# The gate's hidden product ahead of a recurrence, and its values centred as they are turned

## The chip, the cores and the metric

One core of one Trainium2 chip runs the whole program in one launch, all in fp32. The metric is the device time of the launch in microseconds, the median of the runs shown. TensorE multiplies into PSUM (8 banks of 128x512), VectorE (DVE in the rows), ScalarE (ACT) and GpSimd (POOL) do the rest, and SyncE (SP) issues the weight transfers.

## The reference, cut to what matters

The program is a hybrid block (attention and a state-space scan), then two mixers with their feed-forward layers. The change touches the first mixer, RWKV-7 time mixing, on a sequence of 512 with 1024 channels and 16 heads of 64:

```python
xx = token_shift(x) - x
xm = x[None] + xx[None] * mix[:, None, None, :]
...
a = jax.nn.sigmoid(a0 + (xa @ a1) @ a2)
g = jax.nn.sigmoid(xg @ g1) @ g2              # g1: 1024 x 160, g2: 160 x 1024
kk = heads(k * k_k); kk = kk / jnp.maximum(jnp.sqrt(jnp.sum(kk * kk, -1, keepdims=True)), 1e-12)
k = k * (1 + (a - 1) * k_a)
_, y = lax.scan(_wkv7_step, state0, xs)       # y is linear in v
mu = y.mean(-1, keepdims=True)                # over the 64 values of a head
var = jnp.square(y - mu).mean(-1, keepdims=True)
y = ((y - mu) * lax.rsqrt(var + GN_EPS)).reshape(B, S, D) * lnx_g + lnx_b
bonus = jnp.sum(rh * kh * r_k, -1, keepdims=True) * vh
y = (y + bonus.reshape(B, S, D)) * g
return y @ w_o
```

## The kernel before, in words

Activations lie with channels on the partitions: a tile is 128 channels (two heads) by 512 tokens, and eight tiles make one activation. Weights stream from HBM through a ring of six slots of 128x1024 (`ring`, filled by `stream`); `weight_used` counts the chunks that TensorE has finished with and so frees slots in order. Each engine runs a list of instructions in program order, and semaphores join the lists. Between stages all engines meet.

The stages around the change, with their places in the profiled execution:

- r, k, v products and the two hidden products of decay and a (to 801 us). `mixed(dst, diff, branch)` makes the mixed input of one branch on VectorE; `hidden_vector` makes those of branches 3 and 4.
- Preparation (801 to 871 us). Rate products (L1696, L1697) on TensorE, sigmoids on ScalarE, the scan of log decays on VectorE; squares of the keys (L1718), their sums per head (L1700), root (L1723), reciprocal (L1755), spread back over the channels by `spread_heads` (L1630), key normalisation (L1758), scaling of k (L1727, L1760); r times k on GpSimd (L1789) and its sums (L1711); then VectorE operations over a whole activation of 128x4096 (L1762 to L1775).
- Recurrence (871 to 1040 us), chunked: eight chunks of 64 tokens in four pairs. For each pair TensorE turns v, k and b (`turn`, L1863), makes Gram tables, inverts by doubling levels, and forms outputs and states.
- Output stage (1040 to 1141 us). Head means by a product with `head_ones` (L2210), centring (L2268), mixing of branch 5 (L1578), the gate's first product (L2216), squares (L2323), sums (L2222), root (L2342), reciprocal (L2284), spreads (L1630), the gate's second product (L2231, copied to SBUF by L2345), scaling (L2287), bonus added by GpSimd (L2317), the gate multiplied in (L2292, L2296), and the output product w_o (L2254 to L2256). The latter splits every operand into a high and a low half (ScalarE rounds, VectorE subtracts) and makes three passes for each of eight banks in each of eight steps k.

The order of the work is the order in the text: nothing is scheduled at run time.

## Time and profile before

| | us |
|---|---|
| Median of 3 runs (lowest 2231.27, highest 5258.97) | 2231.93 |
| Profiled execution, its time | 2228.96 |
| Its span | 2227.2 |
| TensorE busy in it | 2046.6 (92%) |
| VectorE busy in it | 1298.4 (58%) |
| ScalarE busy in it | 812.3 (36%) |
| GpSimd busy in it | 238.0 (11%) |

The span runs from the first to the last instruction; the time of the execution has 1.8 us more around it. The highest of the three runs is the first one, and the median is not moved by it. Busy shares are averages over stages that are bound by different engines, so they say little of one stage.

### The profile page before, as it was taken

What the parts mean: (1) busy time and instruction counts of PE and PEld (TensorE: products, weight loads), DVE (VectorE), ACT (ScalarE), POOL (GpSimd) and SP (SyncE); (2) the same over time, 40 slices, a digit from 0 to 9 for tenths busy, and PEclk for the clock granted to TensorE, in tenths of its full rate; (3) what the DMA queues carried; (4) which work ended last, traced back from release to release, by engine and by line L of the source; (5) the groups of instructions that cost most, each with busy time, mean ns of one, the idle gap of its engine ahead of it and who ended that gap; (6) DMA issues with size and microseconds to landing.
All of it is one profiled execution on the core that took longest, in us unless ns stands there. A gap on an engine that the chain in (4) does not pass through costs nothing. (4 is left out here: it accounts for less than half of the span.)

```text
span 2227.2 us, 31380 instructions
## 1 busy us (share of the span) xinstructions
PE 2046.6 (92%) x13270; PEld 1546.9 (69%) x13270; DVE 1298.4 (58%) x1845; ACT 812.3 (36%) x1171; POOL 238.0 (11%) x164
## 2 busy tenths in 40 slices
PE   7999989999979973898999999999939899999998
PEld 3877867887858832786567888885516567888885
DVE  2345756666545478676457776434585457666534
ACT  3454654444233362232242222322326533222322
POOL 0000003334410021003200000000035200000000
PEclk9998999999989997999899999999979999999999
DMA  7223002211313210000112222222200022223221
GB/s 281 95 85 105 1 10 69 83 58 58 94 58 112 89 44 1 4 4 21 38 57 101 99 95 95 95 96 82 94 35 1 3 74 85 95 95 101 93 100 38
DMA packets 47019, 158.26 MB, mean 71 GB/s; under 512 B 5328, under 2 KB 7504, under 8 KB 46880
## 3 DMA queue, kind: packets, MB, share of 16 engines
q1 hardware_dynamic: 45296, 151.84, 20.7%
q10 hardware_dynamic: 1584, 4.43, 0.6%
q8 instruction: 105, 1.72, 0.3%
q14 instruction: 34, 0.28, 0.0%
HBM read 154.10 MB, written 2.14 MB: 70 GB/s over the span
## 5 line engine op out<-in xcount | busy, mean ns | idle before, releaser
L1006 PE MATMUL banks<-up_x_high,up_w_high 128*128 128x512 f32 x1056 | 411.5, 390 | 8.4 <-DVE up_w_low L1000 3.8
L1008 PE MATMUL banks<-up_x_high,up_w_low 128*128 128x512 f32 x1056 | 411.0, 389 | 0.0
L1007 PE MATMUL banks<-up_x_low,up_w_high 128*128 128x512 f32 x1056 | 410.9, 389 | 0.0
L1000 DVE TENSOR_TENSOR up_w_low<-weight_ring,up_w_high 128x1024 fp32r<-128x1024 f32 x132 | 161.6, 1225 | 268.6 <-ACT up_w_high L995 268.6
L995 ACT CAST up_w_high<-weight_ring 128x1024 fp32r<-128x1024 f32 x132 | 138.2, 1049 | 362.3 <-PE banks L1008 338.2
L1006 PEld LDWEIGHTS banks<-up_x_high,up_w_high 128*128 128x128 f32 x1056 | 198.2, 188 | 53.2 <-issue 11.6
L1008 PEld LDWEIGHTS banks<-up_x_high,up_w_low 128*128 128x128 f32 x1056 | 198.2, 188 | 41.4
L1007 PEld LDWEIGHTS banks<-up_x_low,up_w_high 128*128 128x128 f32 x1056 | 198.3, 188 | 40.9
L1542 POOL TENSOR_TENSOR hproj_w_low<-weight_ring,hproj_w_high 128x1024 fp32r<-128x1024 f32 x43 | 106.0, 2466 | 498.8 <-ACT hproj_w_high L1342 498.8
L1061 DVE SCALAR_TENSOR_TENSOR act<-banks,cols,act 128x511 f32<-128x511 f32 (+1 forms) x176 | 131.8, 749 | 6.2
L1217 PE MATMUL banks<-hproj_x_high,hproj_w_high 128*128 128x512 f32 x224 | 90.0, 402 | 5.2 <-DVE hproj_x_low L1493 3.4
L425 PE MATMUL banks<-rkv_x_high,rkv_w_high 128*128 128x512 f32 x192 | 75.7, 394 | 13.5 <-DVE rkv_x_low L496 13.3
L1219 PE MATMUL banks<-hproj_x_high,hproj_w_low 128*128 128x512 f32 x224 | 87.9, 393 | 0.0
L1218 PE MATMUL banks<-hproj_x_low,hproj_w_high 128*128 128x512 f32 x224 | 87.9, 392 | 0.0
L1103 ACT ACTIVATE act<-act 128x512 f32<-128x512 f32 x44 | 27.8, 632 | 161.1 <-DVE act L1061 161.1
L449 DVE TENSOR_TENSOR qkv_w_low<-weight_ring,qkv_w_high 128x1024 fp32r<-128x1024 f32 x24 | 29.4, 1225 | 87.3 <-ACT qkv_w_high L445 87.3
L1342 ACT CAST hproj_w_high<-weight_ring 128x1024 fp32r<-128x1024 f32 x44 | 46.0, 1047 | 93.3 <-PE banks L1325 54.4
L426 PE MATMUL banks<-rkv_x_low,rkv_w_high 128*128 128x512 f32 x192 | 75.4, 393 | 0.0
L427 PE MATMUL banks<-rkv_x_high,rkv_w_low 128*128 128x512 f32 x192 | 75.3, 392 | 0.0
L1058 DVE TENSOR_SCALAR act<-banks,cols 128x512 f32<-128x512 f32 x88 | 70.8, 805 | 0.0
L449 DVE TENSOR_TENSOR rkv_w_low<-weight_ring,rkv_w_high 128x1024 fp32r<-128x1024 f32 x24 | 29.3, 1225 | 61.3 <-ACT rkv_w_high L445 61.3
L2641 PE MATMUL banks<-stat,act 128*128 128x128 f32 (+3 forms) x96 | 32.7, 490 | 34.3 <-PEq L2409 27.1
(476 smaller groups left out, 4005.1 us busy)
## 6 DMA issues: line engine op xcount, KB each, us to landing
weight_ring<-in_up SPq DMA_DIRECT2D x88, 512.0 KB, 3.2
weight_ring<-in_down SPq DMA_DIRECT2D x44, 512.0 KB, 3.2
weight_ring<-in_w_ada SPq DMA_DIRECT2D x24, 512.0 KB, 4.5
weight_ring<-in_w_rkv SPq DMA_DIRECT2D x24, 512.0 KB, 3.5
weight_ring<-in_w_in SPq DMA_DIRECT2D x20, 512.0 KB, 3.5
weight_ring<-in_w_out SPq DMA_DIRECT2D x16, 512.0 KB, 3.6
weight_ring<-in_w_q SPq DMA_DIRECT2D x8, 512.0 KB, 5.4
weight_ring<-in_w_k SPq DMA_DIRECT2D x8, 512.0 KB, 3.5
```

What stands on the lines that cost most here:

```text
L425: nc.tensor.matmul(PS[:, n, :], high, x_high[:, parts[s] % slots, :], start=k == 0, stop=False)
L426: nc.tensor.matmul(PS[:, n, :], high, x_low[:, parts[s] % slots, :], start=False, stop=False)
L995: nc.scalar.copy(w_high[:, n % 2, :], ring[:, i % RING, :]).then_inc(wh_made, 1)
L1000: nc.vector.tensor_tensor(w_low[:, n % 2, :], ring[:, i % RING, :], w_high[:, n % 2, :].bitcast(f32), ALU.subtract).then_inc(wl_made, 1)
L1006: nc.tensor.matmul(PS[:, bank, :], high, x_high[:, k, :], start=start, stop=False)
L1007: nc.tensor.matmul(PS[:, bank, :], high, x_low[:, k, :], start=False, stop=False)
L1008: return nc.tensor.matmul(PS[:, bank, :], low, x_high[:, k, :], start=False, stop=stop)
L1061: nc.vector.scalar_tensor_tensor(out=dst(n)[:, j:], in0=PS[:, n % 4, 0:T - j], scalar=w_col(n, taps - 1 - j), in1=dst(n)[:, j:], op0=ALU.m ...
L1217: nc.tensor.matmul(PS[:, bank, :], high, x_high[:, k, :], start=k == 0, stop=False)
L1218: nc.tensor.matmul(PS[:, bank, :], high, x_low[:, k, :], start=False, stop=False)
L1219: return nc.tensor.matmul(PS[:, bank, :], low, x_high[:, k, :], start=False, stop=k == 7)
L1542: nc.gpsimd.tensor_tensor(w_low[:, t % 2, :], ring[:, (first + 1 + t) % RING, :], w_high[:, t % 2, :].bitcast(f32), ALU.subtract).then_inc ...
```

## The change

- The mixed input of branch 5 is made in place of `xx`, behind the mixings of branches 3 and 4. The gate's first product runs in the preparation, behind the key sums; its result goes, unactivated, into the two ring slots that held its weights, and stays there over the recurrence. These slots are given free by the first two gate tiles of the output stage.
- `xx` is also `bonus`, so the squares of the keys get three buffers of their own, and their sums alternate with the rate products. ScalarE's gains wait for the product step that reads what they overwrite. VectorE scales all of k first and normalises the keys after. GpSimd's eight `rk_ones` tables wait for the key sums, since they share memory with the squares' buffers.
- When v is turned, the transposes become products with a matrix that subtracts the mean over each head, so that the recurrence's outputs have mean zero. The means and centring of the output stage go.
- In the output stage the gate is multiplied into y by VectorE from PSUM, ahead of the root, and into the bonus by GpSimd; GpSimd's addition is the last step. The head selector for the square sums is fetched at the recurrence's start.

```diff
-        "pairs64_1", "pairs64_2", "ident64"]
+        "pairs64_1", "pairs64_2", "ident64", "centre"]
...
-           "flip": p + f == P - 1, "neg_after": np.where(f > p, NEG, 0)}
+           "flip": p + f == P - 1, "neg_after": np.where(f > p, NEG, 0), "centre": (p == f) - (p // HD == f // HD) / HD}
...
             for k in range(8):
                 mixed(a_, xx, 3)(k).then_inc(mix_w, 1)
                 mixed(xm, xx, 4)(k).then_inc(mix_a, 1)
+            for k in range(8):
+                mixed(xx, xx, 5)(k)
...
+        gate_step, gate_hidden, gate_kept = sem("gate7_hidden_step"), sem("gate7_hidden_made"), sem("gate7_hidden_kept")
+        hid_g = [ring[0:80, (at["used"] + n) % RING, 0:T] for n in range(2)]
+        key_squares = [late[:, 0:T], late[:, T:2 * T], stat[:, 1, :]]
...
+                def key_sum(n):
+                    pe.wait_ge(key_sq, n + 1)
+                    nc.tensor.matmul(PS[:, 0, :], to_all_groups(n), key_squares[n % 3], start=n == 0, stop=n == 7).then_inc(key_sums, 1)
...
-                for n in range(8):
-                    pe.wait_ge(key_sq, n + 1)
-                    mm = nc.tensor.matmul(PS[:, 0, :], to_all_groups(n), bonus[:, n, :], start=n == 0, stop=n == 7)
-                mm.then_inc(key_sums, 1)
-                pe.wait_ge(inverted, 2)
+                    if n:
+                        key_sum(n - 1)
+                key_sum(7)
+                for n in range(2):
+                    i = at["used"] + n
+                    pe.wait_ge(weight_loaded[i % RING], 16 * (i // RING + 1))
...
+                for k in range(8):
+                    for n in range(2):
+                        mm = nc.tensor.matmul(PS[0:80, 6 + n, :], ring[:, (at["used"] + n) % RING, k * 80:(k + 1) * 80], bonus[:, k, :], start=k == 0, stop=k == 7)
+                    mm.then_inc(gate_step, 1)
+                pe.wait_ge(inverted, 2)
                 for n in range(8):
+                    if n >= 6:
+                        pe.wait_ge(gate_kept, n - 5)
                     spread_heads(n, n).then_inc(spread, 1)
...
-                    nc.scalar.activation(bonus[:, n, :], kk[:, n, :], ACT.Square).then_inc(key_sq, 1)
+                    if n >= 3:
+                        act.wait_ge(key_sums, n - 2)
+                    nc.scalar.activation(key_squares[n % 3], kk[:, n, :], ACT.Square).then_inc(key_sq, 1)
...
-                act.wait_ge(key_sums, 1)
+                act.wait_ge(key_sums, 8)
...
                 for n in range(8):
+                    act.wait_ge(gate_step, n + 1)
                     nc.scalar.activation(bonus[:, n, :], a_[:, n, :], ACT.Identity, scale=col("k_a", n), bias=rest_of_gain[:, n:n + 1]).then_inc(gain_less, 1)
+                for n in range(2):
+                    nc.scalar.copy(hid_g[n], PS[0:80, 6 + n, :]).then_inc(gate_kept, 1)
...
-                act.wait_ge(ends, 1)
...
                 for n in range(8):
+                    dve.wait_ge(gain_less, n + 1)
+                    nc.vector.tensor_tensor(kx[:, n, :], bonus[:, n, :], kx[:, n, :], ALU.mult).then_inc(k_scaled, 1)
+                for n in range(8):
                     dve.wait_ge(spread, n + 1)
                     nc.vector.tensor_tensor(kk[:, n, :], kk[:, n, :], PS[:, n, :], ALU.mult).then_inc(key_unit, 1)
-                    dve.wait_ge(gain_less, n + 1)
-                    nc.vector.tensor_tensor(kx[:, n, :], bonus[:, n, :], kx[:, n, :], ALU.mult).then_inc(k_scaled, 1)
...
+                dve.wait_ge(ends, 1)
...
+                pool.wait_ge(key_sums, 8)
                 for n in range(8):
                     nc.gpsimd.tensor_scalar(rk_ones[:, n * P:(n + 1) * P], mat("head_ones"), col("r_k", n), None, ALU.mult).then_inc(ones_made, 1)
...
-                        mm = nc.tensor.transpose(PS[:, turn_bank(i, n) + p // 4, p % 4 * P:(p % 4 + 1) * P], pair_of(t, i)[:, p, :], mat("ident"))
+                        dst = PS[:, turn_bank(i, n) + p // 4, p % 4 * P:(p % 4 + 1) * P]
+                        if n == 0:
+                            mm = nc.tensor.matmul(dst, pair_of(t, i)[:, p, :], mat("centre"), start=True, stop=True)
+                        else:
+                            mm = nc.tensor.transpose(dst, pair_of(t, i)[:, p, :], mat("ident"))
...
+            @block.sync
+            def _(sp):
+                sp.dma_start(of_heads_late, A["of_heads"]).then_inc(of_in, 16)
...
-                for n in range(8):
-                    nc.tensor.matmul(PS[:, n, :], mat("head_ones"), yy[:, n, :], start=True, stop=True).then_inc(mean_made, 1)
-                pe.wait_ge(gn_centred, 8)
...
-                for k in range(8):
-                    pe.wait_ge(mixed_g, k + 1)
-                    for n in range(2):
-                        mm = nc.tensor.matmul(PS[0:80, 1 + n, :], g[n][:, k * 80:(k + 1) * 80], mix_g[:, k, :], start=k == 0, stop=k == 7)
-                        if k == 7:
-                            mm.then_inc(weight_used, 1)
-                pe.wait_ge(heads_in, 80)
+                pe.wait_ge(of_in, 16)
                 for n in range(8):
                     pe.wait_ge(gn_squared, n + 1)
-                    mm = nc.tensor.matmul(PS[:, 0, :], to_all_groups(n), sq[n], start=n == 0, stop=n == 7)
+                    mm = nc.tensor.matmul(PS[:, 0, :], of_heads_late[:, 2 * (KT - n):2 * (KT - n) + P], sq[n], start=n == 0, stop=n == 7)
...
                 def gate_tile(n):
                     if n >= 4:
                         pe.wait_ge(gate_moved, n - 3)
+                        pe.wait_ge(gn_gated, n - 3)
                     for j in range(2):
-                        mm = nc.tensor.matmul(PS[:, 3 + n % 4, :], g2_[j][:, n * P:(n + 1) * P], hid_g[j], start=j == 0, stop=j == 1)
+                        mm = nc.tensor.matmul(PS[:, 3 + n % 4, :], g2_[j][:, n * P:(n + 1) * P], act_g[j], start=j == 0, stop=j == 1)
+                        if j == 0 and n < 2:
+                            mm.then_inc(weight_used, 1)
...
                 pe.wait_ge(gn_inverted, 1)
+                pe.wait_ge(heads_in, 64)
...
-                    spread_heads((0, 1, 2, 7)[n % 4], n).then_inc(gn_spread, 1)
+                    spread_heads(SPREAD_BANK[n % 4], n).then_inc(gn_spread, 1)
...
                         gate_tile(5 + n // 4 * 2)
...
                         elif k == 0:
                             pe.wait_ge(gate_moved, n + 2)
+                            pe.wait_ge(gn_gated, n + 2)
...
-                nc.vector.tensor_tensor(diff[:, :, 1:T], x[:, :, 0:T - 1], x[:, :, 1:T], ALU.subtract).then_inc(differed, 1)
-                nc.vector.tensor_scalar(diff[:, :, 0:1], x[:, :, 0:1], -1.0, None, ALU.mult).then_inc(differed, 1)
-                for n in range(8):
-                    dve.wait_ge(mean_made, n + 1)
-                    nc.vector.scalar_tensor_tensor(out=yy[:, n, :], in0=PS[:, n, :], scalar=-1.0 / HD, in1=yy[:, n, :],
-                                                   op0=ALU.mult, op1=ALU.add).then_inc(gn_centred, 1)
-                dve.wait_ge(differed, 2)
-                for k in range(8):
-                    mixed(mix_g, diff, 5)(k).then_inc(mixed_g, 1)
...
+                def times_gate(n):
+                    dve.wait_ge(gate_moved, n + 1)
+                    dve.wait_ge(gn_squared, n + 1)
+                    if n >= 6:
+                        dve.wait_ge(gn_scaled, n + 1)
+                    nc.vector.scalar_tensor_tensor(out=yy[:, n, :], in0=PS[:, 3 + n % 4, :], scalar=col("lnx_g", n), in1=yy[:, n, :],
+                                                   op0=ALU.mult, op1=ALU.mult).then_inc(gn_gated, 1)
+
+                def times_root(n):
+                    dve.wait_ge(gn_spread, n + 1)
+                    if n < 6:
+                        dve.wait_ge(gn_gated, n + 1)
+                    nc.vector.tensor_tensor(yy[:, n, :], yy[:, n, :], PS[:, SPREAD_BANK[n % 4], :], ALU.mult).then_inc(gn_scaled, 1)
...
-                for n in range(8):
-                    dve.wait_ge(gn_spread, n + 1)
-                    nc.vector.scalar_tensor_tensor(out=yy[:, n, :], in0=yy[:, n, :], scalar=col("lnx_g", n), in1=PS[:, (0, 1, 2, 7)[n % 4], :],
-                                                   op0=ALU.mult, op1=ALU.mult).then_inc(gn_scaled, 1)
-                    if n >= 2:
-                        dve.wait_ge(gn_shifted, n - 1)
-                        dve.wait_ge(gate_moved, n - 1)
-                        nc.vector.tensor_tensor(yy[:, n - 2, :], yy[:, n - 2, :], gate[:, n - 2, :], ALU.mult).then_inc(gated, 1)
-                for n in range(6, 8):
-                    dve.wait_ge(gn_shifted, n + 1)
-                    dve.wait_ge(gate_moved, n + 1)
-                    nc.vector.tensor_tensor(yy[:, n, :], yy[:, n, :], gate[:, n, :], ALU.mult).then_inc(gated, 1)
-                    if n == 6:
-                        low_of_input(0)
+                for n in range(4):
+                    times_gate(n)
+                for n in range(4):
+                    times_root(n)
+                times_gate(4)
+                times_gate(5)
+                for n in range(4, 8):
+                    times_root(n)
+                low_of_input(0)
+                times_gate(6)
+                times_gate(7)
                 low_of_input(1)
...
-                for n in range(8):
+
+                def gate_bonus(n):
                     pool.wait_ge(bonus_shifted, n + 1)
+                    pool.wait_ge(gate_moved, n + 1)
+                    nc.gpsimd.tensor_tensor(bonus[:, n, :], bonus[:, n, :], gate[:, n, :], ALU.mult).then_inc(bonus_gated, 1)
+
+                def add_bonus(n):
+                    pool.wait_ge(bonus_gated, n + 1)
                     pool.wait_ge(gn_scaled, n + 1)
-                    nc.gpsimd.tensor_tensor(yy[:, n, :], yy[:, n, :], bonus[:, n, :], ALU.add).then_inc(gn_shifted, 1)
+                    pool.wait_ge(gn_gated, n + 1)
+                    nc.gpsimd.tensor_tensor(yy[:, n, :], yy[:, n, :], bonus[:, n, :], ALU.add).then_inc(gated, 1)
+
+                for at0, at1 in ((0, 4), (4, 6), (6, 8)):
+                    for n in range(at0, at1):
+                        gate_bonus(n)
+                    for n in range(at0, at1):
+                        add_bonus(n)
...
-                    act.wait_ge(gn_centred, n + 1)
                     nc.scalar.activation(sq[n], yy[:, n, :], ACT.Square, scale=HD ** -0.5).then_inc(gn_squared, 1)
...
+                def move_gate(n):
+                    act.wait_ge(gate_out, n + 1)
+                    nc.scalar.copy(gate[:, n, :], PS[:, 3 + n % 4, :]).then_inc(gate_moved, 1)
+
+                for n in range(2):
+                    nc.scalar.activation(act_g[n], hid_g[n], ACT.Sigmoid).then_inc(hid_g_taken, 1)
+                act.wait_ge(hid_g_taken, 2)
+                act.wait_ge(gn_eps, 1)
                 high_of_weights(0)
                 high_of_weights(1)
-                act.wait_ge(weight_used, first_g + 2)
-                for n in range(2):
-                    nc.scalar.activation(hid_g[n], PS[0:80, 1 + n, :], ACT.Sigmoid).then_inc(hid_g_taken, 1)
-                act.wait_ge(gn_eps, 1)
                 act.wait_ge(gn_sums, 1)
                 nc.scalar.activation(head_sums, PS[:, 0, :], ACT.Sqrt, bias=small[:, 250:251]).then_inc(gn_rooted, 1)
-                for n in range(8):
-                    act.wait_ge(gate_out, n + 1)
-                    nc.scalar.copy(gate[:, n, :], PS[:, 3 + n % 4, :]).then_inc(gate_moved, 1)
+                for n in range(6):
+                    move_gate(n)
                 high_of_input(0)
+                move_gate(6)
+                move_gate(7)
                 high_of_input(1)
...
-                for dst, src, landed in ((of_heads, A["of_heads"], heads_in), *((t, A["to_heads"], heads_in) for t in to_heads),
-                                         (g2_[0], A["w_g2"][0:80, :], g2_in), (g2_[1], A["w_g2"][80:160, :], g2_in)):
+                for dst, src, landed in ((g2_[0], A["w_g2"][0:80, :], g2_in), (g2_[1], A["w_g2"][80:160, :], g2_in),
+                                         *((t, A["to_heads"], heads_in) for t in to_heads)):
```

## Rows read from the trace of the kernel before

**Rows 1.** The table by stretch, us of the span: each engine's busy time (instructions), clock, DMA.
```profile
801.20:816.70 15.50, 12.27 (x41) 4.67 (x42) 13.65 (x19) 14.91 (x26) 7.47 (x8) 1.00 0.15 60
...
842.50:871.00 28.50, 2.73 (x4) 0.50 (x2) 28.04 (x18) 3.76 (x2) 5.38 (x1) 0.59 0.00 0
...
900.00:1039.90 139.90, 124.58 (x4200) 112.46 (x4201) 91.68 (x140) 42.55 (x63) 8.28 (x8) 1.00 0.02 4
...
1094.00:1100.00 6.00, 5.91 (x14) 4.73 (x15) 1.04 (x2) 0.00 (x0) 0.00 (x0) 0.50 0.01 3
```

**Rows 2.** Timeline of TensorE: start, us, line, tiles, count, idle before and its releaser.
```profile
1039.93 7.11 PE L2210 MATMUL banks<-act,squares 128*128 128x512 f32 x16 [0.93 <-PEq L1843]
1050.47 13.93 PE L2216 MATMUL banks<-act,weight_ring 128*80 128x512 f32 x32 [3.44 <-DVE act L1578]
...
1071.10 7.03 PE L2231 MATMUL banks<-act 80*128 80x512 f32 x16
1078.06 1.14 PE L1630 MATMUL banks<-aux 16*128 16x512 f32 x8
...
1082.77 2.24 PE L1630 MATMUL banks<-aux 16*128 16x512 f32 x8
1084.94 5.87 PE L2231 MATMUL banks<-act 80*128 80x512 f32 x8
1094.09 0.77 PE L2254 MATMUL banks<-w_o_x_high,w_o_w_high 128*128 128x512 f32 x1 [3.29 <-DVE w_o_x_low L2279]
```

**Rows 3.** Timeline of ScalarE in the same stretch.
```profile
1045.51 1.83 ACT L2323 ACTIVATE aux<-act 128x512 f32<-128x512 f32 x3 [5.89 <-DVE act L2268]
...
1050.23 1.98 ACT L2329 CAST w_o_w_high<-weight_ring 128x1024 fp32r<-128x1024 f32 x2
1052.22 1.28 ACT L2339 ACT_TABLE_LOAD   x1
...
1072.64 0.69 ACT L2342 ACTIVATE aux<-banks,small 128x512 f32<-128x512 f32 x1
```

**Rows 4.** Groups by line between 1039.9 and 1094 us: count, busy us, mean ns, idle before.
```profile
L2313 POOL TENSOR_SCALAR w_out_act<-w_out_act,cols 128x512 f32<-128x512 f32 x8 | 19.8, 2496 | 5.1 <-POOLq L1843 5.1
...
L2287 DVE SCALAR_TENSOR_TENSOR act<-act,cols,banks 128x512 f32<-128x512 f32 x8 | 5.7, 738 | 2.5 <-PE banks L1630 2.5
...
L2275 DVE TENSOR_TENSOR w_o_w_low<-weight_ring,w_o_w_high 128x1024 fp32r<-128x1024 f32 x2 | 2.8, 1420 | 0.0
```

**Rows 5.** Single lines of GpSimd in the whole span: duration min/median/max in ns.
```profile
L2313 POOL TENSOR_SCALAR w_out_act<-w_out_act,cols x8: 1556/2072/5803, 1039.9 to 1057.1; 128x512 f32<-128x512 f32 x8
...
L2317 POOL TENSOR_TENSOR act<-act,w_out_act x8: 1267/1712/1728, 1080.1 to 1091.0; 128x512 f32<-128x512 f32 x8
```

**Rows 6.** Timeline of VectorE before the recurrence.
```profile
794.79 0.75 DVE L1578 SCALAR_TENSOR_TENSOR act<-w_out_act,cols,act 128x512 f32<-128x512 f32 x1
...
822.45 3.35 DVE L1755 RECIPROCAL aux<-aux 128x512 f32<-128x512 f32 x1
...
829.77 1.39 DVE L1760 TENSOR_TENSOR act<-w_out_act,act 128x512 f32<-128x512 f32 x1
...
842.44 4.41 DVE L1762 TENSOR_TENSOR w_out_act<-w_out_act,act 128x4096 f32<-128x4096 f32 x1
846.77 1.27 DVE L1764 COPY late<-rkv_act 128x64 f32<-128x64 f32 x1
```

**Rows 7.** Timelines of ScalarE, TensorE and GpSimd before the recurrence.
```profile
800.33 0.58 ACT L1662 COPY aux<-banks 64x512 f32<-64x512 f32 x1
...
815.89 0.79 ACT L1721 ACTIVATE w_out_act<-banks,cols 128x512 f32<-128x512 f32 x1
...
812.85 7.13 PE L1700 MATMUL banks<-w_out_act,aux 128*128 128x512 f32 x16
...
829.34 1.27 POOL L1789 TENSOR_TENSOR w_out_act<-act 128x512 f32<-128x512 f32 x1 [20.56 <-DVE act L1760]
```

**Rows 8.** Timeline of TensorE at the recurrence's first turn.
```profile
875.02 1.09 PE L1863 MATMUL banks<-squares,act 128*128 128x128 f32 x8
```

26 lines of the change are left out of this document (13 added, 13 removed).

## The prediction

> **What bounds the kernel now.** I read the table by stretch first. The recurrence (900 to 1040 us) is TensorE's: 124.6 us busy of 139.9 at a clock of 1.00. The stretch ahead of it (842.5 to 871 us) is VectorE's, 28.04 us of 28.5 [rows 1]. Between recurrence and output product I then followed TensorE's timeline, and there the reader is to see a chain rather than one busy engine: the head means at 1039.93, the gate's first product from 1050.47 for 13.93 us, the square sums behind it, four gate tiles at 1071.10, head spreads at 1078.06 and 1082.77, the last gate tiles at 1084.94, and the first output matmul at 1094.09 after 3.29 us of waiting for VectorE's low half of the input [rows 2]. That is 1094.09 - 1039.93 = 54.2 us. TensorE's order is fixed, so what stands ahead of the square sums delays root, reciprocal and all else. Nothing runs beside this chain that could fill it, so a cut of the chain shows in full at the end.
>
> **The output stage after the change (the gain).** I walk through it from 1039.9.
> ScalarE can square at once, since the values arrive centred: 8 x 0.60 (three take 1.83) ends at 1044.7; then a table load of 1.28, two sigmoids of about 0.55 straight from the ring, 1047.1; two weight halves, 1.98, 1049.1; a second table load, 1.28, and the root, 0.69: 1051.1 [rows 3].
> TensorE sums squares as they come, one 128x512 sum being two passes of 7.11/16 = 0.444 us: 8 x 0.87 from 1040.6 is 1047.5. Four gate tiles at 7.03/4 = 1.76 end at 1054.5 [rows 2].
> VectorE has nothing to do until the halves are there: two low halves of 1.42 on average end at 1051.2, and the reciprocal, 3.35, ends at 1054.6 [rows 4, 6]. It meets TensorE just as gate tile 3 ends. The first four spreads take 1.1 [rows 2]: 1055.7.
> VectorE then makes four gate products and four root products. Both read one operand from PSUM, as L2287 does (0.74 each, issued every 0.65) [rows 4]: gate products to 1057.2, root products to 1059.7. TensorE meanwhile makes gate tiles 4 and 5 to 1059.2, spreads 4 to 7 to 1060.7 (the last waits for root product 3), gate tiles 6 and 7 to 1064.2. VectorE's products 4, 5 and roots 4 to 7 end at 1063.3.
> GpSimd gets a job that decides more than before: eight shifts, eight products of bonus and gate (moved to it), eight additions. Shifts at the uncontended 1.56 take until 1052.4, and 1 us more for the two low halves: 1053.4. A product or addition takes 1.27 when nothing competes, 1.71 when VectorE does [rows 5]. At 1.3, four products end at 1058.6 and the first addition at 1059.9; ScalarE rounds it (0.6), and VectorE's low half follows its last root product, 1063.3 + 0.6 to 1.3. Everything is late together: the output product starts at about 1064.5. For k = 1, 2, 3 GpSimd is ready by 1064, for 4 and 5 by 1069, for 6 and 7 by 1075; the product needs them over 5 us apart (24 passes of at least 5.91/28 = 0.21) [rows 1], so only the first counts. At 1.71 the start is 1.4 to 2 us later.
> So 1094.1 - 1064.5 = 29.6 us. What is late next is TensorE itself, then VectorE. Removed and paid in this sum: means, centring, mixing (VectorE) and the 13.93 us product. DMA moves: the two gate weights are issued ahead of the head selectors instead of behind, and land well before 1047; ring slots come free at gate tile 0, some 15 us earlier than now, so no weight chunk is later.
> **The clock there.** Today it has fallen by the last gate tiles (four passes per tile, 5.87 us for two tiles against 3.5) and is 0.50 for the first 6 us of the output product [rows 1, 2]: the level of 1.2 GHz. The 14 passes there took 5.9 us; at 2.4 GHz they take half, so 2.9 are lost. The light spell ahead of the fall (spreads, 2.24 us with a wait) is 1.6 us in the new order and follows another as now. I call the clock even: the fall costs 2.4 on the tiles (start 1067) and the 2.9 stay; no fall gives the 2.9 back. Ends 27.2 and 32.5, I take 29.
>
> **Ahead of the recurrence (a cost).** VectorE's eight more mixings go behind 794.79: 8 x 0.66 ends at 800.8, while ScalarE's last copy of that stage ends at 800.91 [rows 6, 7]. Free by 0.1 us; without that cover at most 5.3.
> Key sums now alternate with the rate products, 0.87 + 0.86 on TensorE per tile, against ScalarE's three operations every 1.68; ScalarE ends this loop at 816.7 [rows 7]. The squares wait for a buffer three tiles back, which TensorE frees about 1.8 us early. The sums end near 816.4 instead of 820, but VectorE is busy to 822 with the scans and the centring, and its reciprocal starts at 822.45 [rows 6]: nothing gained, up to 1 lost if the loop drags.
> The gate product, 13.93 us, runs from 816.7 to 830.6 on a TensorE that idles there. Behind it wait ScalarE's eight gains (they overwrite its input; the last 831.2) and the spreads; behind the gains, VectorE's eight key products. VectorE is at 825.8 then, and it is not held by them alone: GpSimd multiplies each scaled key at once. The row pair to see: GpSimd's L1789 runs 829.34 to 830.61, and VectorE's L1760, issued at 829.77, takes 1.39 instead of 0.69, ending 0.55 behind it [rows 6, 7]. The two exclude each other. Today VectorE's PSUM product of 0.6 hides under GpSimd's, so the pair costs 1.9 and eight end at 842.4. After: key products alone lock step with GpSimd at 1.27 + 0.6 = 1.87, ending near 838.5; then eight PSUM products of 0.6, 843.3, under which GpSimd ends. Copy L1764 no longer waits for GpSimd (1.27 to 0.25) [rows 6]. Balance 0.9 - 1.0 = 0. If instead VectorE runs through before GpSimd gets in, it is held by the gains only: 831.8, then 836.6, 5.8 earlier.
> GpSimd's r_k tables, eight in 7.47 us [rows 1], move from under the scans to 816.4, beside VectorE's centring, as long as L1762's 4.41: one wait of 0.93 ahead of it and one behind, or none. I take +1 for this stage; ends -6 and +5.
> The Trainium skill bears here (SBUF — State Buffer, "SBUF: two separate sides"): VectorE with two SBUF inputs and a GpSimd operation that reads SBUF take a shared port pair, whole instructions long; with one SBUF input outside its two-port modes VectorE does not contend. This trace agrees: 0.74 for L2287 with GpSimd busy [rows 4]. A rule that each GpSimd operation blocks is against this change, which adds eight; my fourth case prices it.
>
> **In the recurrence (a cost).** 32 transposes, eight in each of four turns, become products with the centring matrix. Eight transposes take 1.09 [rows 8]. Two passes of 128 columns, from 0.444 for 512, are 0.22: eight take 1.78. +0.7 to 0.8 per turn, 3.0 if TensorE's chain carries all, 0 if slack does (it idles 15 of 139.9 us) [rows 1]. I take 2.3; should weight loads not overlap, 4 x 3 = 12 is the far end. The selector's DMA is issued at the recurrence's start on an idle queue, 72 KB: 0. The matrix makes the constants 64 KB longer, fetched behind the early ones: 0 to 0.3. Dropping ScalarE's wait for the chunk ends frees it 7 us early, for nobody.
>
> **Sum.** -29 + 1 + 2.3 = -25.7. On the profiled execution, 2228.96 us: 2203.3. The median of the runs is 2231.93, 3 above it: 2206.
>
> **The rivals.** (1) Clock kept and VectorE never locked: 2231.9 - 32.5 - 3 + 2.3 = 2199; for it, TensorE has no gap over 1 us in my walk; against it, today's fall after the same pattern. (2) The clock falls early: all four late gate tiles at 1.2 GHz, 3.5 each. Then 1055.7 + 7.0 + 2.2 + 7.0 = 1072, 22 gained, 3.3 and perhaps 3 lost: 2213 to 2216. (3) Centring costs its far end, 12 in place of 2.3: 2216. (4) The other side, slower than before: GpSimd's port. If every GpSimd operation stopped VectorE for its whole length ahead of the recurrence (7.5 + 8 x 1.27 = 17.7, and the last held for 4.4 by a long one of VectorE's, 22.1), and took 2.5 in the output stage, as the shifts do today, the start would be 1040 + 13 x 2.5 + 1.3 = 1073.8, 20.3 gained: 2231.9 - 20.3 + 22.1 + 2.3 = 2236 [rows 4]. It decides once stalls take over 26 us in all; against it, L1760's loss is half of a GpSimd operation today. (5) The change gives nothing because something else ends the stage, such as weights in the ring: 2232 to 2235; against it, the slots free earlier.
>
> **How the numbers follow.** Forecast 2206 (2201 to 2211) 0.47; (1) 0.19; (2) 0.18; (3) 0.07; (4) 0.04; (5) 0.05. The range 2195 to 2219 takes in both ends of the clock and nearly all of the port question, and leaves out (4), (5). Two per cent, 44.6 us, is about what a measurement of this kernel can tell from no change; no case reaches it, as even 32.5 + 6 is 1.7%. Faster by more 0.02, within 0.96, slower by more 0.02.
>
> **What would show it.** Output matmul 24 to 30 us after the recurrence's end instead of 54; square sums done 7.6 after it; reciprocal and gate tile 3 ending together; GpSimd's first addition at about +20. Turn 0 of each pair at 1.8 instead of 1.09. Key products in steps of about 1.87. I am wrong if the first output matmul waits for GpSimd, if the clock row behind the last spreads is 0.5, or if VectorE stands idle between 826 and 845.

## The result and the profile after

| | before | changed |
|---|---|---|
| Median, us (runs) | 2231.6 (4) | 2205.07 (4) |
| The changed kernel's runs | | 2195.43, 2200.32, 2209.82, 2212.37 |
| Ratio, 95% interval | | 0.9879 [0.9857, 0.9902] |
| Profiled execution, span | 2228.96, 2227.2 | 2200.32, 2198.5 |

The change gains 1.2%: the median falls by 26.5 us to 2205.07 (forecast 2206). One thing of the table is odd: 39 more runs of the kernel before, made beside the experiments, lie in one group from 2227.3 to 2236.3; the four of the changed kernel span 17 us, in two pairs. The profiled execution is one of the lower pair.

The table by stretch of the changed kernel (ahead of the recurrence, recurrence, output stage up to the output product, output product, all that follows) answers to [rows 1]:

```profile
799.60:868.10 68.50, 42.97 (x112) 15.00 (x112) 64.98 (x55) 33.27 (x42) 22.17 (x16) 0.81 0.04 14
869.40:1040.60 171.20, 152.07 (x4864) 136.10 (x4864) 109.66 (x166) 52.38 (x76) 8.30 (x8) 0.98 0.02 4
1040.60:1064.80 24.20, 23.38 (x64) 9.49 (x64) 15.88 (x20) 15.17 (x23) 24.13 (x17) 1.00 0.31 81
1064.80:1107.80 43.00, 42.97 (x190) 35.62 (x191) 19.07 (x21) 10.51 (x14) 11.55 (x8) 1.00 0.26 86
...
1107.80:2198.50 1090.70, 1024.49 (x4286) 767.92 (x4284) 641.44 (x1042) 365.52 (x564) 58.82 (x69) 0.97 0.23 76
```

The output stage is TensorE's now, busy 23.38 of 24.2 us at a clock of 1.00, and GpSimd is busy for 24.13 of them. Measured between the same instructions, in us of each profiled execution (1.5 us lie between the stretch and the recurrence, in both):

| | before | changed | difference |
|---|---|---|---|
| start of the stretch ahead of the recurrence | 801.2 | 799.6 | -1.6 |
| that stretch | 69.0 | 68.3 | -0.7 |
| recurrence | 168.3 | 171.3 | +3.0 |
| its end to the first output matmul | 54.1 | 24.1 | -30.0 |
| output product | 45.7 | 43.0 | -2.7 |
| all that follows, untouched | 1087.4 | 1090.7 | +3.3 |

The sum is -28.7. The last row is instructions that nobody changed: over the thirteen profiled executions of this document it lies between 1087.2 and 1091.5, so its +3.3 is scatter from one execution to the next; here it goes with the clock, 0.98 before and 0.97 after over the same 4286 matmuls. The first row holds the eight added mixings on VectorE, which end at 799.24, just ahead of ScalarE's last copy at 799.31. The stretch begins between 797.2 and 801.5 in the profiled executions without these mixings and between 797.4 and 801.4 in those with them, so this row is scatter too, and the rows that the change touched add up to -30.4.

TensorE's timeline of the output stage, beside [rows 2], whose first output matmul stood 54.2 us behind the first row:

```profile
1041.41 2.81 PE L2245 MATMUL banks<-aux,late 128*128 128x512 f32 x6 [1.68 <-ACT aux L2366]
1044.06 1.88 PE L2245 MATMUL banks<-late 128*128 128x512 f32 x4
...
1048.35 7.03 PE L2255 MATMUL banks<-act 80*128 80x512 f32 x16
1055.31 1.14 PE L1630 MATMUL banks<-aux 16*128 16x512 f32 x8
1056.38 3.70 PE L2255 MATMUL banks<-act 80*128 80x512 f32 x8
1060.01 1.14 PE L1630 MATMUL banks<-aux 16*128 16x512 f32 x8
1061.08 3.70 PE L2255 MATMUL banks<-act 80*128 80x512 f32 x8
1064.83 0.47 PE L2282 MATMUL banks<-w_o_x_high,w_o_w_high 128*128 128x512 f32 x1
```

Means and gate product are gone from it; no row waits except the first; the last gate tiles take 3.70 where they took 5.87, and the first output matmul 0.47 where it took 0.77. Those two are the clock that stayed up. VectorE and GpSimd in the same stretch:

```profile
1051.41 3.35 DVE L2318 RECIPROCAL aux<-aux 128x512 f32<-128x512 f32 x1
...
1063.79 0.78 DVE L2299 TENSOR_TENSOR w_o_x_low<-act,w_o_x_high 128x512 fp32r<-128x512 f32 x1
```
```profile
1040.67 13.51 POOL L2344 TENSOR_SCALAR w_out_act<-w_out_act,cols 128x512 f32<-128x512 f32 x8 [4.54 <-POOLq L1867]
1054.15 4.96 POOL L2349 TENSOR_TENSOR w_out_act<-w_out_act 128x512 f32<-128x512 f32 x4
1059.07 4.96 POOL L2355 TENSOR_TENSOR act<-act,w_out_act 128x512 f32<-128x512 f32 x4
1063.99 2.98 POOL L2349 TENSOR_TENSOR w_out_act<-w_out_act 128x512 f32<-128x512 f32 x2
```

The low part of the input (L2299) is the last thing that the output product needs from another engine. Here it ends at 1064.57, 0.2 us before TensorE is through with its gate tiles, so nothing waits. It reads two tiles of the core's memory and starts 0.24 us before one run of GpSimd operations ends. Keep this pair of rows in mind: the experiments trace the two groups of times to it.

### The profile page after: what moved, and what is told of

Its sections match the earlier page's. It is cut to its first block and busy times, and to the rows that moved or that the text cites. A ratio compares the mean times of both kernels' runs of the same rounds, so it can differ in the third digit from the quotient of the medians.

```text
span 2198.5 us, 31439 instructions
## 1 busy us (share of the span) xinstructions
PE 2038.5 (93%) x13286; PEld 1547.9 (70%) x13286; DVE 1282.0 (58%) x1835; ACT 814.6 (37%) x1173; POOL 242.7 (11%) x172
```

## The experiments

"Stage" is the time from the recurrence's end to the first output matmul. Times are medians; the profiled execution has the stretches.

| kernel | us (lowest to highest, runs) | recurrence | stage | output product |
|---|---|---|---|---|
| gate half alone | 2204.15 (2203.53 to 2205.47, 4) | 166.5 | 34.0 | 42.9 |
| centring half alone | 2229.27 (2223.95 to 2236.21, 10) | 170.9 | 51.2 | 45.8 |
| the same, sums first | 2232.95 (2229.21 to 2234.86, 10) | 171.2 | 51.7 | 45.4 |
| mean not subtracted | 2197.68 (2194.38 to 2208.34, 4) | 166.4 | 26.7 | 43.0 |
| before, TensorE kept busy | 2236.61 (2227.6 to 2244.74, 10) | 168.0 | 67.6 | 43.3 |
| query x key on VectorE | 2207.9 (2197.43 to 2209.1, 4) | 171.4 | 31.4 | 45.3 |
| shifts twice | 2221.76 (2221.36 to 2223.28, 4) | 171.5 | 43.8 | 45.9 |
| shifts early | 2203.89 (2203.36 to 2205.17, 4) | 173.7 | 26.5 | 43.0 |
| pauses | 2200.72 (2197.46 to 2204.09, 4) | 172.1 | 24.1 | 43.0 |
| pauses, query x key on VectorE | 2199.78 (2198.32 to 2201.11, 4) | 169.7 | 25.6 | 42.9 |
| pauses, spare products | 2202.31 (2200.68 to 2203.89, 4) | 170.0 | 24.1 | 43.0 |

### The two halves of the change

The gate half alone: transposes as before, means by products, centring by VectorE in the output stage.

```diff
-                        if n == 0:
-                            mm = nc.tensor.matmul(dst, pair_of(t, i)[:, p, :], mat("centre"), start=True, stop=True)
+                for n in range(8):
+                    nc.tensor.matmul(PS[:, n, :], mat("head_ones"), yy[:, n, :], start=True, stop=True).then_inc(mean_made, 1)
+                pe.wait_ge(gn_centred, 8)
```

> Only the first half of the change: the gate's hidden product is made ahead of the recurrence, v is turned by transposes as before, and the head means and their subtraction are back in the output stage. Theory (the output stage is one chain, and each piece counts by its place in it): TensorE makes the means for 7.1 us, squares follow VectorE's centring, and the square sums end about 14.2 us into the stage instead of 7.7; everything behind moves by the same 6.5 to 7, so the stage from its start to the first output matmul takes about 31 us (24.2 with the whole change, 54.2 before), and the recurrence is back at 168.2 us. The median is about 4 us above that of the whole change, near 2209. Rival (the two halves cover each other: with the product gone, the means fall under waits that exist anyway): the stage stays within 1 us of 24.2 and the time falls by 3 us against the whole change, since only the cost in the recurrence goes.

The centring half alone, on the kernel before:

```diff
-                for n in range(8):
-                    nc.tensor.matmul(PS[:, n, :], mat("head_ones"), yy[:, n, :], start=True, stop=True).then_inc(mean_made, 1)
-                pe.wait_ge(gn_centred, 8)
+                        if n == 0:
+                            mm = nc.tensor.matmul(dst, pair_of(t, i)[:, p, :], mat("centre"), start=True, stop=True)
```

> Only the second half of the change: v is centred as it is turned, the means and their subtraction are gone from the output stage, and the gate's hidden product stays there. Theory (chain): the product now waits for VectorE's difference, 4.43 + 0.57, and the first mixing instead of the centring, so it starts about 5.7 us into the stage instead of 10.5 and all behind it moves by 4.9; the stage takes 49.3 us, the recurrence 171.2, and the sum is about -2 us against before. Rival (means and centring are worth their own length, 7.1 + 4.9 us): stage near 42 us, about -9 us in all.

TensorE in the first:

```profile
1035.80 8.80 PE L2241 MATMUL banks<-act,squares 128*128 128x512 f32 x16 [0.93 <-PEq L1867]
1045.43 2.81 PE L2246 MATMUL banks<-aux,late 128*128 128x512 f32 x6 [0.83 <-issue]
```

and in the second:

```profile
1044.33 15.72 PE L2217 MATMUL banks<-act,weight_ring 128*80 128x512 f32 x32 [6.82 <-DVE act L1578]
```

The gate half carries the gain: stage 34.0 against 54.1. By the medians it carries all of it: 2204.15 against the whole change's 2205.07, both 0.9879 of before, and not the 4 us more that were expected. Its four runs lie within 1.9 us, where the whole change's fall in two groups.

The means take 8.80 us here (7.11 in [rows 2]), for they begin at the low clock; less those 1.7 us the stage is 32.3, where the first theory gave 31.

The centring half by itself gives 2.9 us in the output stage and takes 2.6 in the recurrence: its ratio to before is 0.999 [0.9976, 1.0005]. The gate product comes only 4.7 us sooner after the recurrence (5.8 for 10.5) and, after TensorE has idled 6.82 us, runs its first part at the low clock, 15.72 us for 13.93. Nothing that is removed ahead of VectorE's mixing pays while the gate product waits for that mixing.

In the stage the two halves are worth more together: once the gate product is gone, centring takes it from 34.0 to 24.1, and pays 4.8 of these 9.9 us back in the recurrence (166.5 against 171.3). The profiled spans differ by 3.6 (2202.1 and 2198.5), no more than the scatter of the last row; in the changed kernel's median even this is lost to its upper group.

Could the centring half pay by another order? Square sums and root ahead of the gate product and its sigmoid, on the centring half alone:

```diff
+                    mm = nc.tensor.matmul(PS[:, 0, :], to_all_groups(n), sq[n], start=n == 0, stop=n == 7)
                 for k in range(8):
                     pe.wait_ge(mixed_g, k + 1)
...
-                    mm = nc.tensor.matmul(PS[:, 0, :], to_all_groups(n), sq[n], start=n == 0, stop=n == 7)
```

> As centre_only, and TensorE makes the square sums ahead of the gate's hidden product, with ScalarE's root ahead of its sigmoids. Theory (a good part of the change's gain is the order, which frees root and reciprocal, not the work moved): the sums end 7.7 us into the stage, the reciprocal is ready at about 15 instead of 37, but the gate tiles still wait for the product (21.5) and the sigmoids, so the stage is then product, eight gate tiles of 1.76, spreads: 21.5 + 2 + 14 + 2 + some 3 of additions, about 41 to 43 us. That would be 7 us better than centre_only by the order alone. Rival (the work moved is all that counts): the stage stays within 1 us of centre_only's 49.

```profile
1047.24 5.35 PE L2216 MATMUL banks<-aux 128*128 128x512 f32 x6 [5.02 <-DMA aux<-in_to_heads]
...
1056.72 13.90 PE L2222 MATMUL banks<-act,weight_ring 128*80 128x512 f32 x32
1071.78 3.70 PE L2232 MATMUL banks<-act 80*128 80x512 f32 x8 [1.17 <-ACT act L2338]
```

No: the ratio is 1.0008 [0.9998, 1.0017], and the theory's 41 to 43 us for the stage fell. The sums wait 5.02 us for the head selectors' transfer, begin at the low clock, and push the gate product to 1056.72, so that the gate tiles begin at 1071.78. That is 28.6 us behind the recurrence's end, as in the centring half alone (28.3), and from there both need 23 more. The changed kernel avoids both: it loads one selector in the recurrence, and has no gate product there.

### What centring costs

The changed kernel with transposes in the turns; the mean is then never subtracted, and the output is another one.

> The changed kernel with transposes in place of the centring products when v is turned, so the mean over a head is not subtracted at all: the output differs, the number of instructions in the output stage does not. Theory (TensorE's chain carries the centring in full): the recurrence takes 168.2 us instead of 171.2, every other stage is as in the changed kernel, and the median is 3 us lower, near 2202. Rival (something else took the 3 us, such as a stall of the new queue at the recurrence's start): the recurrence stays above 170.5 us.

TensorE at the first turn of values in the changed kernel (eight products, each two instructions), and at the next turn, eight transposes as ever:

```profile
872.98 2.05 PE L1889 MATMUL banks<-squares,act 128*128 128x128 f32 x16
...
876.87 1.09 PE L1891 MATMUL banks<-squares,act 128*128 128x128 f32 x8
```

Four such turns are 4 x 0.96 = 3.8 us. The recurrences agree in size: seven kernels with centring (those of the table but two, which add work at its start, and the changed kernel) take 169.7 to 172.1, mean 171.2; four without (before, before kept busy, gate half, mean not subtracted) 166.4 to 168.3, mean 167.3. The difference of the means is 3.9, but it mixes two kinds of kernel. With the gate product in its old place centring costs some 3 us (168.2 to 171.1, two kernels each); with the product moved ahead it costs some 4.7 (166.5 to 171.2, two against five).

TensorE's busy time in the recurrence, by the same table of stretches, is 151.74 on average with centring and 147.26 without, 4.5 more. So centring costs some 3 to 5 us, about the TensorE time that it adds, and how much of that time slack hides isn't shown. The stage of this kernel is 26.7 because its square sums began at the low clock (4.48 us for the first six instructions, where the changed kernel takes 2.81) and because its low part took 1.69, for which TensorE waited 0.96:

```profile
1034.33 4.48 PE L2242 MATMUL banks<-aux,late 128*128 128x512 f32 x6 [1.68 <-ACT aux L2363]
...
1060.33 0.47 PE L2279 MATMUL banks<-w_o_x_high,w_o_w_high 128*128 128x512 f32 x1 [0.96 <-DVE w_o_x_low L2296]
```

### Whether the clock was the gain

On the kernel before, spare products after head spreads 4 to 7 and ahead of the output product:

```diff
                     spread_heads((0, 1, 2, 7)[n % 4], n).then_inc(gn_spread, 1)
+                    if n >= 4:
+                        pe.wait_ge(gate_moved, 5)
+                        nc.tensor.matmul(PS[:, 3, :], mat("ones"), squares[:, 0:T], start=True, stop=True)
...
+                for _ in range(4):
+                    nc.tensor.matmul(PS[:, 3, :], mat("ones"), squares[:, 0:T], start=True, stop=True)
```

> The kernel before, with spare products (their results are never read) that keep TensorE busy while it waits for gate tiles and ahead of the output product; nothing of the change is in it. Theory: part of what the change gained, 5.3 us, was not work removed but the granted clock kept at 1.00, which fell before in gate tiles 6 and 7 (5.87 us each where others take 3.5 to 3.7) and in the first blocks of the output product (45.7 us where 43.0 is its length at full clock). With the pauses filled the output product takes 43.0 and the whole gets 3 to 5 us shorter than before: 2227 to 2229. Rival: the clock fell for another reason than the pauses, then tiles 6 and 7 still take 5.87 and the whole is within 1 us of before, or above it, since the spare products cost 0.2 to 0.4 each.

The granted clock is the third number from the end of each row; then TensorE:

```profile
1070.00:1080.00 10.00, 10.00 (x30) 4.15 (x29) 5.50 (x5) 4.40 (x7) 1.39 (x2) 1.00 0.00 0
1080.00:1090.00 10.00, 10.00 (x16) 2.44 (x14) 8.03 (x9) 0.82 (x2) 8.59 (x6) 0.73 0.01 2
1090.00:1095.00 5.00, 5.00 (x7) 1.73 (x7) 1.35 (x2) 0.00 (x0) 2.38 (x2) 0.50 0.00 0
```
```profile
1082.30 1.13 PE L2243 MATMUL banks<-squares 128*128 128x512 f32 x2
...
1088.22 2.07 PE L2243 MATMUL banks<-squares 128*128 128x512 f32 x2
...
1094.09 7.03 PE L2231 MATMUL banks<-act 80*128 80x512 f32 x8
```

The theory fell as it was put: the time is 1.0019 [1.0001, 1.0037] of before. TensorE had no pause between 1080 and 1095 by the records, and the granted clock sank to 0.50 (1.2 GHz) all the same. At that level the spare products, 2.07 each, stood on the path and the stage took 67.6. The output product did take 43.3 instead of 45.7, since by its second matmul the clock was back (0.40 each, where the kernel before began with 0.63). So 2.4 us of it do hang on the clock, and 42.9 to 43.3 stands in every row of the table whose clock is up there. Why it sank while TensorE was busy I leave open; only its consequence is shown.

### The two groups of times

These runs began with another aim, the port that VectorE and GpSimd share. The eight products of query and key on VectorE, between its key products:

```diff
-                    nc.gpsimd.tensor_tensor(bonus[:, n, :], r[:, n, :], kx[:, n, :], ALU.mult).then_inc(rk_made, 1)
...
+                    nc.vector.tensor_tensor(bonus[:, n, :], r[:, n, :], kx[:, n, :], ALU.mult).then_inc(rk_made, 1)
```

> The changed kernel with the eight products of query and key (the first factor of the bonus) made by VectorE between its own key products in place of GpSimd. Theory: in the stretch ahead of the recurrence VectorE and GpSimd hinder each other while both read and write the core's memory; the key products took 1.43 each beside GpSimd, and with GpSimd silent they take about 0.6 to 0.7 and the added ones as much, so that 16 operations take 10 to 11 us where 8 took 11.45: the stretch ends 0.5 to 2 us earlier, and the whole gains as much. Rival: they don't hinder each other and 1.43 is the operation's own length: then 16 take 22 us and the stretch gets 10 us longer.

Ahead of the recurrence the theory held: sixteen products end at 834.67, where eight took from 824.94 to 836.39, each 0.68 once GpSimd's last table (its L1818, until 825.93) is out of the way; the stretch takes 66.7 instead of 68.3. But the stage took 31.4. VectorE, GpSimd and TensorE there:

```profile
1062.16 8.09 DVE L2304 TENSOR_TENSOR w_o_x_low<-act,w_o_x_high 128x512 fp32r<-128x512 f32 x1
1070.18 1.40 DVE L2311 SCALAR_TENSOR_TENSOR act<-banks,cols,act 128x512 f32<-128x512 f32 x2
```
```profile
1057.41 4.97 POOL L2360 TENSOR_TENSOR act<-act,w_out_act 128x512 f32<-128x512 f32 x4
1062.34 2.49 POOL L2354 TENSOR_TENSOR w_out_act<-w_out_act 128x512 f32<-128x512 f32 x2
1064.78 2.48 POOL L2360 TENSOR_TENSOR act<-act,w_out_act 128x512 f32<-128x512 f32 x2
1067.22 2.48 POOL L2354 TENSOR_TENSOR w_out_act<-w_out_act 128x512 f32<-128x512 f32 x2
1071.09 2.97 POOL L2360 TENSOR_TENSOR act<-act,w_out_act 128x512 f32<-128x512 f32 x2 [1.38 <-DVE act L2311]
```
```profile
1070.51 0.77 PE L2287 MATMUL banks<-w_o_x_high,w_o_w_high 128*128 128x512 f32 x1 [7.36 <-DVE w_o_x_low L2304]
```

The low part took 8.09 us instead of 0.78. It was issued at 1062.16, 0.2 us before one GpSimd operation ended, and got in neither there nor between any of the next six, whereas the changed kernel's, issued 0.24 us before the same operation's end, did get in; it ended at 1070.25, 0.55 us after GpSimd ran out of work at 1069.70, and GpSimd had run out only because its next addition needed VectorE's L2311, which stood behind the low part.

The output product starts 7.3 us late and, TensorE having idled 7.36 us, at the low clock (0.77 for the first matmul): 45.3 for 43.0. Together that is 9.6 us, most of the distance between this kernel's one run at 2197.43 and its three at 2207.8 to 2209.1; the changed kernel's two pairs stand 13.2 apart, more than this stall by itself gives. This is the only profile of an upper run.

Each of these low parts ends 0.55 us behind the end of some GpSimd operation: in the changed kernel, the gate half, the shifts made early and the kernel whose mean isn't subtracted behind the first that ends after it was issued (0.78 or 1.7 us in all), here behind the seventh. So the change from one GpSimd operation to the next is sometimes met and sometimes not; what decides it isn't shown.

GpSimd's shifts made twice, so that its row of work is 12.3 us longer (the norm's shift is then in the output twice):

```diff
+                pool.wait_ge(bonus_shifted, 8)
+                for n in range(8):
+                    nc.gpsimd.tensor_scalar(bonus[:, n, :], bonus[:, n, :], col("lnx_b", n), None, ALU.add).then_inc(bonus_shifted, 1)
...
-                    pool.wait_ge(bonus_shifted, n + 1)
+                    pool.wait_ge(bonus_shifted, n + 9)
```

> The changed kernel with GpSimd's eight shifts of the bonus made twice over (so the norm's shift is added twice to the output). They take 13.5 us for eight beside VectorE in the output stage. Theory: the first gated addition, which the output product waits for by way of its input, ended some 3 us ahead of need, so another 12.5 to 13.5 us of GpSimd delay the output product by about 10: from the end of the recurrence to it 33 to 35 us in place of 24.2, and the whole 9 to 11 us longer. This tells how near the changed kernel stands to the next bound. Rival: the gated additions are far from the path; the stage keeps its 24.2 and the time is that of the changed kernel.

```profile
1073.73 10.85 DVE L2299 TENSOR_TENSOR w_o_x_low<-act,w_o_x_high 128x512 fp32r<-128x512 f32 x1 [9.51 <-ACT w_o_x_high L2380]
```

The low part was ready to start at 1073.73, 32.7 us after the recurrence: the slack theory's 33. Then it stood 10.85 us. GpSimd worked without a gap from 1041.02 to 1084.03; the low part ended at 1084.58, 0.55 us behind it, as before. So the stage was 43.8 and not 33 to 35, and the median 16.7 us above the changed kernel's and not 9 to 11: the theory had the slack right and no stall in it. The four runs lie within 1.9 us, which fits a stall in each of them; one was profiled.

The shifts at the recurrence's start, where GpSimd idles:

```diff
             def _(pool):
+                for n in range(8):
+                    nc.gpsimd.tensor_scalar(bonus[:, n, :], bonus[:, n, :], col("lnx_b", n), None, ALU.add).then_inc(bonus_shifted, 1)
                 for c in range(NCH):
...
-                for n in range(8):
-                    nc.gpsimd.tensor_scalar(bonus[:, n, :], bonus[:, n, :], col("lnx_b", n), None, ALU.add).then_inc(bonus_shifted, 1)
```

> The changed kernel with GpSimd's eight shifts made at the recurrence's start, where GpSimd is idle, in place of the output stage. Theory: GpSimd isn't what bounds the output stage now, TensorE's square sums and gate tiles are, so the stage stays within 0.5 us of 24.2 and the whole within 1 us of the changed kernel, unless VectorE, less hindered in the output stage, makes the centre shorter by up to 2 us. Rival: the stage hangs on GpSimd, and gets 3 us or more shorter; or the shifts hinder VectorE at the recurrence's start, and the first 15 us of the recurrence get 1 to 3 us longer.

The stage isn't GpSimd's: it got no shorter. That it is 26.5 us and not within 0.5 of 24.2 comes from square sums at the low clock (1.5 more) and a wait of 0.95 for the first low part. The four runs lie within 1.8 us. GpSimd now waits for gate tiles between its first products, but the row in which the low part is issued (1067.78) has no pause from 1061.50 on; it took 1.68 us and got in at the next change of operation. The recurrence takes 2.4 us longer than the changed kernel's (173.7): VectorE's products at its start, beside the shifts, are 0.8 of it, and the granted clock over its first 24 us is 0.79 where that kernel has 0.86.

Then the direct test, with nothing taken from GpSimd but three pauses:

```diff
                 def gate_bonus(n):
+                    if n in (4, 6):
+                        pool.wait_ge(xol_made, n // 2 - 1)
...
                 def add_bonus(n):
+                    if n == 6:
+                        pool.wait_ge(xol_made, 3)
```

> The changed kernel in which GpSimd stops three times until VectorE has made a low part of the output product's input: before the gatings 4 and 6 and before the additions of tiles 6 and 7. Nothing is taken away. Theory: the changed kernel's runs fall in two groups (2195 and 2200, 2210 and 2212) since VectorE's first low part, which reads two tiles in the core's memory, has to find a gap in a row of GpSimd operations without a pause; where it misses it, it stands for 8 to 11 us (0.7 by itself), the output product starts 7 us late and at half the clock. With a pause made for it every run finds it: all within 5 us, median 2195 to 2201, stage 24 to 25 us. Rival: the two groups come from something else (the clock, transfers): then they stay, with a median at 2203 to 2210.

```profile
1065.19 0.78 DVE L2299 TENSOR_TENSOR w_o_x_low<-act,w_o_x_high 128x512 fp32r<-128x512 f32 x1
```
```profile
1060.44 4.97 POOL L2359 TENSOR_TENSOR act<-act,w_out_act 128x512 f32<-128x512 f32 x4
1066.05 2.54 POOL L2351 TENSOR_TENSOR w_out_act<-w_out_act 128x512 f32<-128x512 f32 x2 [0.63 <-DVE w_o_x_low L2299]
```

GpSimd waits 0.63 us, the stage keeps its 24.1, and no run is in the upper group: 2197.46 to 2204.09, ratio 0.9858 [0.9843, 0.9873]. Counted over kernels: without pauses in GpSimd's row (the changed kernel, mean not subtracted, query x key on VectorE) 6 of 12 runs are in an upper group at 2207.8 to 2212.4; with pauses 0 of 12 are. The 4.4 us at the median are less certain, since the two ratios' intervals overlap.

Two things keep this from being the whole account. The gate half and the kernel with the shifts early have an unbroken row at their low part too, and none of their 8 runs is in an upper group. And the runs of the centring half lie over 12 us and those of the kernel kept busy over 17 us, though the low parts in their profiles take 0.68 and 0.69 us; where that scatter comes from wasn't looked into. The pauses remove a stall that is seen in two traces, and with it, as far as 12 runs can tell, the upper group; the stall isn't seen in an upper run of the changed kernel itself.

The two other kernels with the pauses. With the query-key products on VectorE:

> The same pauses of GpSimd, and the eight products of query and key made by VectorE in place of GpSimd as in the run before, where the stretch ahead of the recurrence took 66.7 us in place of 68.3 while the output stage had the long stall. Theory: the stall goes and the 1.6 us stay: median 1 to 2.5 us under that of the kernel with the pauses alone, 2194 to 2199. Rival: without the stall the two are equal, because the clock at the recurrence's start takes the 1.6 us back.

The stretch ahead keeps its 66.7, the stall is gone, and the four runs lie at 2198.32 to 2201.11, ratio 0.9856 [0.9839, 0.9872]. The 0.9 us at the median are less than four runs can tell. The stage is 25.6 because the first six square sums take 4.40 us, at the low clock again, and the recurrence is 2.4 shorter than with the pauses alone; neither was sought. Its median is the lowest of the kernels here whose output is right.

With spare products ahead of the recurrence:

```diff
+                pe.wait_ge(prepared, 5)
+                pe.wait_ge(bonus_made, 1)
+                for _ in range(5):
+                    nc.tensor.matmul(PS[:, 0, :], mat("ones"), squares[:, 0:T], start=True, stop=True)
```

> The kernel with the pauses, and five spare products on TensorE between its last work ahead of the recurrence and the recurrence's first products (it idled 22.7 us there and began at a granted clock of 0.50, held for some 3.5 us). Theory: the recurrence begins at the full clock and its first products take half: 1 to 2 us less in the recurrence, the median 1 to 2 us under that of the kernel with the pauses alone. Rival: the gain is nothing, as the clock dips at 883 to 890 us come earlier or deeper, or the spare products run into the start and delay it by up to 1 us.

```profile
865.77 7.33 PE L1732 MATMUL banks<-squares 128*128 128x512 f32 x10 [17.16 <-DVE w_out_act L1804]
874.35 0.29 PE L1881 MATMUL banks<-act,w_out_act 64*64 64x128 f32 x1 [1.24 <-PEq L1837]
```

The first products take 0.29 instead of 0.44, so the clock was up, and the recurrence is 2.1 shorter than with the pauses alone. But the spare products, at the low clock at first, end at 873.1, and the recurrence starts 3.1 later than it would have. The rival held: nothing gained, with a delay of 3.1 us where it allowed for 1.

## Why the prediction was right, and where it was not

**The output stage (-29).** Right in its parts and its sum: 24.1 us against the 24.6 that the walk gave. Counted from the recurrence's end: square sums done at 7.7 (7.6 forecast), root at 10.7 (11.2), reciprocal at 14.1 (14.7) beside gate tile 3 at 14.7 (14.6), first addition at 19.7 (20.0), first low part from 23.1 (23.4). TensorE was next to be late, as put.

**The clock (called even).** This was the term with the wrong size. It stayed at 1.00 throughout: 2.2 us on the last gate tiles and 2.7 on the output product, so that stage and product together gave 32.7, the end of 32.5. What I had against it, that a light spell like that of before would let it fall again, didn't come: between 1041.41 and 1064.83 TensorE has no pause over 0.1. Whether that is the reason stays open, since the kernel kept busy had none either and its clock fell.

**Ahead of the recurrence (+1).** Measured -0.7. The lock step with GpSimd was there, but in steps of 1.67 us where I took 1.87, and only for the last six key products: the first two, made while GpSimd was still at its tables, took 0.7 each. So the key products end at 836.4 and not 838.5 (a query on their line gives the least, median and longest of them in ns; the rest is VectorE's timeline):

```profile
L1779 DVE TENSOR_TENSOR act<-w_out_act,act x8: 628/1751/1753, 824.9 to 834.6; 128x512 f32<-128x512 f32 x8
```
```profile
824.94 11.45 DVE L1779 TENSOR_TENSOR act<-w_out_act,act 128x512 f32<-128x512 f32 x8
836.31 4.86 DVE L1782 TENSOR_TENSOR act<-act,banks 128x512 f32<-128x512 f32 x8
...
845.54 0.23 DVE L1786 COPY late<-rkv_act 128x64 f32<-128x64 f32 x1
```

The copy took 0.23 (0.25 forecast), GpSimd's tables 9.44 beside the long centring, mixing and gate product were hidden as put. The query-key kernel shows that 1.6 us were left in this lock step.

**In the recurrence (+2.3).** Too small: +3.0 between the two profiled executions, some 3 or 4.7 between kernels that differ in little else. A product's two instructions cost 0.26, not 0.22, so that four turns add 3.8 us and not 3.0; that slack would take a part of it isn't borne out. The far end of 12 and rival (3) are out.

**The sum.** By the profiled execution 2203.3 was forecast and 2200.3 came; the terms measured, -1.6 - 0.7 + 3.0 - 32.7 + 3.3, add up to the -28.7. So the terms that the change touched gave 30.4 us where 25.7 were forecast, and scatter elsewhere took 1.7 of the 4.7 back. Rival (1) had the clock right, though not its unlocked VectorE; its 2199 is counted from the median, and from the same execution it would be 2195.8, further off than the forecast.

That the median is 2205.07 and agrees with 2206 is in part luck: a clock called even, which stayed up, was set off by a stall that the forecast didn't have, and the median is the middle between two groups, neither of which is there. Rival (4) priced GpSimd's port as whole GpSimd operations that stop VectorE, 26 us in all. The price was wrong, but the place of the mechanism was nearly right: one VectorE operation stands behind a whole row of them, for 8 us, in the one upper run that was profiled. My walk had both engines' rows in it and asked only how long each operation takes beside the other, not whether one finds a gap.

The Trainium skill (SBUF — State Buffer, "SBUF: two separate sides") says that the shared port pair goes to whichever starts first, for the whole instruction. The run with 8.09 us agrees that the operation is stopped fully, and goes beyond it: at the end of the instruction that was running the waiting VectorE operation didn't get in, but another six instructions of GpSimd did.

## What to carry to other kernels

Where GpSimd works without a pause beside VectorE, look at each VectorE operation that reads two tiles of the core's memory and has somebody waiting for it: give it a pause by a wait of GpSimd on its result, a wait of 0.63 us here, after which no run of 12 was in the upper group, where 6 of 12 had been. When a kernel's runs scatter more after a change than before, treat the scatter as a finding and profile a run of each group. And a chain pays only from where it is cut: centring at the turn gave nothing that can be measured (0.999) while the gate product stood behind it, and 9.9 us in the stage, less 4.8 in the recurrence, once that was gone; and in the medians even these 5 us show only where the stall is away (2200.72 with the pauses, 2204.15 without centring, with intervals that overlap).

## What the runs showed of the hardware that had not been expected

- A VectorE operation of 0.7 us that reads two tiles beside an unbroken row of GpSimd operations took 8.09 and 10.85 us, and ended 0.55 us after GpSimd's last one, both times. In four other profiles with such a row it took 0.78 or 1.7 us and ended as long behind the first GpSimd operation that ended after it was issued. With operations that read one of their tiles from PSUM (L2306, L2313) nothing like it is in any run: a row of them beside the same GpSimd operations went on every 0.66 and 0.62 us.
- TensorE's granted clock fell to 0.73 and then 0.50 over a stretch in which the records show it busy without a pause (1080 to 1095 us in the kernel kept busy).
- Eight 128x128 fp32 products of 128 columns take 2.05 us where eight transposes of the same tiles take 1.09.
- The same 4286 matmuls behind the output product took 1087.2 to 1091.5 us from one execution to the next, so a difference of 3 us between two profiled spans says nothing by itself.
